# Attention by head pairs: both heads' logits alternate in pieces of 256 keys, six probability slots, pairwise waits

## What is computed

```
even: ya = sliding_window_sink_attn(aq, ak, av, sinks, slopes[:6])   # 6 heads, 2 kv heads, window 128, sink in the softmax
      yb = moba_attn(bq, bk, bv, slopes[6:])                         # 6 heads, at this length plain causal with slope * distance
      ym = memory_cross_attn(mq, mk, mv)                             # 4 heads, 256 memory keys
odd:  yc = forgetting_attn(cq, ck, cv, cf + b_f)                     # 12 heads, causal, bias from a cumulative sum
      ym = memory_cross_attn(mq, mk, mv)                             # 4 heads
both: y = concatenate(...) * silu(z);  x = x + y @ w_out
```

## Time and profile before

| | |
|---|---|
| median of 3 runs | 1302.41 us |
| profiled execution | 1304.05 us |
| its span | 1302.2 us |
| PE (matmul) busy | 1256.6 us, 97% |
| DVE busy | 640.7 us, 49% |
| ACT busy | 570.8 us, 44% |
| POOL busy | 132.2 us, 10% |
| chain that ended last | PE 93%, DVE 3%, ACT 2%, issue 1%, DMA 1% |

### The profile page before, as it was taken

One profiled execution on the slowest core, in us unless ns is written; L12 is line 12 of the kernel. 1 busy time (PEld: TensorE's weight loads), 2 busy tenths in 40 slices (PEclk: granted clock), 3 DMA queues, 4 the chain that ended last, 5 costly groups with the idle time before them and its releaser, 6 DMA issues.

```text
span 1302.2 us, 17223 instructions
## 1 busy us (share of the span) xinstructions
PE 1256.6 (97%) x6858; PEld 1014.4 (78%) x6858; DVE 640.7 (49%) x1265; ACT 570.8 (44%) x1026; POOL 132.2 (10%) x146
## 2 busy tenths in 40 slices
PE   5999999999999999999989999999799999999998
PEld 4887888889867777888978886666797889566688
DVE  4485232885343444345376637554336652445531
ACT  4433322333344455333356656554225663555520
POOL 1000000000000000000000072211300005031322
PEclk9999999999999999999989999999899999999999
DMA  5332223332312212325243321111222332021121
GB/s 170 115 98 83 95 92 96 97 98 88 98 33 65 65 33 90 119 98 178 65 98 97 95 67 34 33 44 55 65 72 92 97 98 90 24 90 57 33 67 63
DMA packets 119047, 105.77 MB, mean 81 GB/s; under 512 B 17836, under 2 KB 115500, under 8 KB 118968
## 3 DMA queue, kind: packets, MB, share of 16 engines
q1 hardware_dynamic: 117320, 98.46, 24.7%
q10 hardware_dynamic: 1648, 6.23, 1.3%
HBM read 102.55 MB, written 2.12 MB: 80 GB/s over the span
## 4 chain that ended last, share of the span: by engine, by line
PE 93%; DVE 3%; ACT 2%; issue 1%; DMA 1%; SPq 0%; DVEq 0%; ACTq 0%
PE acc L1385 26%; PE acc L1386 24%; PE acc L1387 24%; PE acc L1695 7%; PE aux L1726 3%; PE aux L1708 2%; PE aux L1539 2%; PE aux L1553 1%; ACT whi L583 1%; DVE wlo L912 1%; PE acc L1699 1%; DMA xrow<-x_dram 0%; PE aux L1603 0%; PE aux L1602 0%; PE aux L1456 0%
## 5 line engine op out<-in xcount | busy, mean ns | idle before, releaser
L1385 PE MATMUL acc<-ht_hi,whi 128*128 128x512 f32 x864 | 355.1, 411 | 8.4 <-DVE wlo L912 4.3
L1386 PE MATMUL acc<-ht_lo,whi 128*128 128x512 f32 x864 | 338.5, 392 | 0.0
L1387 PE MATMUL acc<-ht_hi,wlo 128*128 128x512 f32 x864 | 338.4, 392 | 0.0
L912 DVE TENSOR_TENSOR wlo<-raw,whi 128x2048 fp32r<-128x2048 f32 x71 | 163.4, 2304 | 148.9 <-ACT whi L583 148.8
L1385 PEld LDWEIGHTS acc<-ht_hi,whi 128*128 128x128 f32 x864 | 162.8, 188 | 67.9 <-issue 31.2
L1387 PEld LDWEIGHTS acc<-ht_hi,wlo 128*128 128x128 f32 x864 | 163.2, 189 | 35.1
L1386 PEld LDWEIGHTS acc<-ht_lo,whi 128*128 128x128 f32 x864 | 163.5, 189 | 29.7 <-issue 1.9
L583 ACT ACTIVATE whi<-raw 128x2048 fp32r<-128x2048 f32 x71 | 135.3, 1909 | 64.3 <-DMA raw<-o_w_mem_kv_dram 35.7
L529 POOL TENSOR_SCALAR whi<-raw 128x512 fp32r<-128x512 f32 x64 | 43.1, 673 | 1103.2 <-DMA raw<-e_w_in_dram 768.5
L1385 PE MATMUL acc<-whi,ht_hi 128*128 128x256 f32 x416 | 117.9, 283 | 0.0
L1386 PE MATMUL acc<-wlo,ht_hi 128*128 128x256 f32 x416 | 117.7, 283 | 0.0
(11 more groups left out here) (217 smaller groups left out, 1855.6 us busy)
## 6 DMA issues: line engine op xcount, KB each, us to landing
raw<-w_in_dram SPq DMA_DIRECT2D x72, 512.0 KB, 4.6
raw<-o_w_in_dram SPq DMA_DIRECT2D x28, 512.0 KB, 4.8
raw<-e_w_in_dram SPq DMA_DIRECT2D x18, 512.0 KB, 4.9
raw<-w_proj_pool_dram SPq DMA_DIRECT2D x8, 512.0 KB, 3.9
raw<-w_proj_mlstm_dram SPq DMA_DIRECT2D x8, 512.0 KB, 4.0
raw<-w_out_dram SPq DMA_DIRECT2D x8, 512.0 KB, 4.1
raw<-o_w_out_dram SPq DMA_DIRECT2D x8, 512.0 KB, 5.1
raw<-e_w_in_dram SPq DMA_DIRECT2D x12, 256.0 KB, 4.1
```

Of the source, the lines that this page charges most:

```text
L912: v.tensor_tensor(wlo[:, slot, :], raw[:, slot, :], whi[:, slot, :].bitcast(F32), ALU.subtract).then_inc(w_split, 1)
L1385: mm(out_, w_hi_, x_hi, start=first, stop=False)
L1386: mm(out_, w_hi_, x_lo, start=False, stop=False)
L1387: return mm(out_, w_lo_, x_hi, start=False, stop=last)
```

## The change

The loop runs over 32 pairs of jobs instead of 64 jobs. TensorE's iteration p: the logits of both heads of pair p, in pieces of at most 256 keys, a piece of the one head and a piece of the other in turn, each head in its own PSUM bank; one z product; the turning of both heads of pair p - 2; the second z product; the values of pair p - 3. It waits for both minima (memory heads: both exponentials) of pair p - 1 before the logits of pair p. VectorE makes the sink sums and inverses of a pair with one instruction each, ahead of the next pair's minima instead of behind them, and a memory pair's minima with one reduce. ScalarE scales pair p - 1 before it makes the exponentials of pair p. `pr` has six slots in place of four; `prT` is placed anew for each layer, and three constant tiles are moved to make room. Tiles 3 to 5 of the output product are also taken into the end of the loop, a pair's turning and values in between. The core of the diff:

```diff
-        pr = at("pr", [P, 4, S], R0 + 4 * K)
+        pr = at("pr", [P, 6, S], R0 + 4 * K)
...
-        def logit_bank(i):
-            return acc[:, 2 + i % 2, :]
+        def logit_bank(e):
+            return acc[:, 2 + e, :]
...
+        def pr_slot(p, e):
+            return 2 * (p % 3) + e
...
# ScalarE
+                for p in range(NP + 5):
...
+                    if z_due(p) is not None:
...
+                        nc.scalar.activation(zT[:, hu % 2, :], acc[:, hu % 2, :], ACT.Tanh, scale=0.5).then_inc(th_ready, 1)
+                    if 1 <= p <= NP:
+                        k = p - 1
+                        act.wait_ge(ri_ready, pairs_done + k + 1)
+                        for e, job in enumerate(pairs[k]):
+                            tile = pr[:, pr_slot(k, e), 0:job.keys]
+                            nc.scalar.activation(tile, tile, ACT.Copy,
+                                                 scale=stats[:, 4, 2 * k + e:2 * k + e + 1]).then_inc(norm_ready, 1)
+                    if p < NP:
+                        for e, job in enumerate(pairs[p]):
+                            i = 2 * p + e
+                            act.wait_ge(nm_ready, 2 * pairs_done + i + 1)
...
+                            nc.scalar.activation(tile, tile if job.bias is not None else logit_bank(e)[:, 0:job.keys], ACT.Exp,
+                                                 scale=-1.0, bias=stats[:, 1, i:i + 1],
+                                                 accum_out=stats[:, 2, i:i + 1]).then_inc(pr_ready, 1)
...
# VectorE
+                for p in range(NP + 6):
+                    if 1 <= p <= NP:
+                        k = p - 1
+                        dve.wait_ge(pr_ready, 2 * (done + k + 1))
+                        i = 2 * k
+                        if pairs[k][0].sink is not None:
+                            dve.wait_ge(es_ready, i + 2)
+                            step(v.tensor_tensor(stats[:, 2, i:i + 2], stats[:, 2, i:i + 2], stats[:, 3, i:i + 2], ALU.add))
+                        v.reciprocal(stats[:, 4, i:i + 2], stats[:, 2, i:i + 2]).then_inc(ri_ready, 1)
+                    if p < NP:
+                        g = done + p
+                        if pairs[p][0].bias is None:
+                            dve.wait_ge(logit_ready, g + 1)
+                            keys = pairs[p][0].keys
+                            v.tensor_reduce(stats[:, 1, 2 * p:2 * p + 2], acc[:, 2:4, 0:keys], AX.X,
+                                            ALU.min).then_inc(nm_ready, 2)
...
# TensorE
+                def logits(p):
+                    if p:
+                        pe.wait_ge(nm_ready if pairs[p - 1][0].bias is not None else pr_ready, 2 * (done + p))
+                    first = pairs[p][0]
+                    forget = first.bias is not None and first.bias[0] == "forget"
+                    for c in range(0, first.keys, 2 * P):
+                        w = min(2 * P, first.keys - c)
+                        for e, job in enumerate(pairs[p]):
+                            (qt, qp), (kt_, kp) = job.q, job.k
+                            k0 = P * job.k0 + c
+                            ins = mm(logit_bank(e)[:, c:c + w], qk[qp:qp + HD2, qt, P * job.t:P * job.t + P],
+                                     (mkT if job.bias is None else qk)[kp:kp + HD2, kt_, k0:k0 + w],
+                                     start=True, stop=not (forget and c + w == job.keys))
...
+                def turn(k):
+                    if done + k:
+                        pe.wait_ge(prT_copied, done + k)
+                    for e, job in enumerate(pairs[k]):
+                        pe.wait_ge(norm_ready, 2 * (done + k) + e + 1)
+                        for b in range(job.keys // P):
+                            ins = nc.tensor.transpose(trans_bank(e)[:, P * b:P * b + P],
+                                                      pr[:, pr_slot(k, e), P * b:P * b + P], ident[:])
+                    ins.then_inc(prT_ready, 1)
...
+                for p in range(NP + 3):
+                    if p < NP:
+                        logits(p)
+                        z_product(2 * p)
+                    if 2 <= p < NP + 2:
+                        turn(p - 2)
+                    if p < NP:
+                        z_product(2 * p + 1)
+                    elif p < NP + 2:
+                        if p == NP:
+                            pe.wait_ge(acc_free, a_out)
+                            pe.wait_ge(pr_ready, 2 * (done + NP))
+                        first = 3 * (p - NP)
+                        rows_as_tiles_come(n_out, a_out, n_out % SLOTS, a_out % 2, op_hi, op_lo, 32 + 8 * L,
+                                           range(first, first + 3))
+                    if p >= 3:
+                        weighted(p - 3)
+                done += NP
+                rows_stage(name + "_out", op_hi, op_lo, 32 + 8 * L, 1 if L == 0 else None, 6)
```

More of the change, by code:

```diff
@@ L853, in _ @@
                 az = plan[name + "_z"][1]
-                jobs = JOBS[L]
-                for i in range(len(jobs) + 7):
-                    if L == 0 and i == 52:
+                pairs = PAIRS[L]
+                for p in range(NP + 5):
+                    if L == 0 and p == 26:
                         act.dma_start(memrow[:], memv).then_inc(mem_in, 16)
[L860 to L881, removed]
+                    if z_due(p) is not None:
+                        hu = z_due(p)
                         act.wait_ge(acc_ready, 2 * az + hu + 1)
@@ L1729, in _ @@
-                done += len(jobs)
-                rows_stage(name + "_out", op_hi, op_lo, 32 + 8 * L, 1 if L == 0 else None, 3)
+                def logits(p):
[5 more added lines that the diff above has]
+                        w = min(2 * P, first.keys - c)
+                        for e, job in enumerate(pairs[p]):
+                            (qt, qp), (kt_, kp) = job.q, job.k
[3 more added lines that the diff above has]
+                                     start=True, stop=not (forget and c + w == job.keys))
+                    if forget:
+                        for e, job in enumerate(pairs[p]):
+                            ins = mm(logit_bank(e)[:, job.keys - P:job.keys], ident_r[:], causal_r[:], start=False, stop=True)
+                    ins.then_inc(logit_ready, 1)
@@ new lines, in weighted @@
+                def weighted(k):
+                    pe.wait_ge(prT_copied, done + k + 1)
+                    job = pairs[k][0]
+                    j, nb = k // TT, job.keys // P
+                    if job.t == 0 and (L or j >= 2):
+                        pe.wait_ge(t_ready, 31 + 8 * L + j)
+                    for b in range(nb):
+                        for e, one in enumerate(pairs[k]):
+                            ins = mm(out_bank(j)[HD2 * e:HD2 * e + HD2, P * job.t:P * job.t + P],
+                                     (mv if job.bias is None else vv)[:, job.k0 + b, one.v:one.v + HD2],
+                                     prT[L][2 * (k % 2) + e][:, P * b:P * b + P], start=b == 0, stop=b == nb - 1)
+                    ins.then_inc(o_ready, 1)
```

142 lines of the change are left out of this document (62 added, 80 removed).

## The result

The changed kernel takes 1252.26 us (median of 4 runs, 1250.65 to 1254.13), the kernel before 1303.01 beside it (1302.07 to 1303.86). The ratio is 0.9612, 95% interval 0.96 to 0.9624. The forecast was 1253.0 with 1244 to 1282. The profiled execution of after took 1254.13, with a span of 1252.3; before it was 1304.05 and 1302.2.

What follows compares the result with a forecast made beforehand. TensorE was taken to bound the loops through the order of its work; 25 + 30.5 - 2.3 - 1 + 1.5 - 4.5 = 49.2 off the profiled 1304.05 gives 1254.9, 1253 as a median of runs, range 1244 to 1282.

Steps and rivals of the forecast that it cites:

- Fewer changes of use: TensorE's order in both attention loops: three changes per pair instead of five, 0.39 saved in each of 64 pairs, 25 us.
- Two heads beside each other: Logits in both loops: the two heads' row halves run at a time, 143 steps x 0.213, 30.5 us saved.
- halves in turn: Rival on the logits: the two heads' passes don't overlap, 21 us of gain stay, about 1281; chance 0.13.
- Alternation costs: Rival on the logits: each pass that changes head pays a full change of use, 0.2, about 1334; chance 0.04.
- Weight loads: Logits pieces of 128 keys: four loads in a row outlast the overlapped passes, at most 4.5, half taken: 2.3 us lost.
- The rounds of DVE and ACT: Both loops: ACT's 2.95 and DVE's 2.8 per pair stay below TensorE's 3.26; the rival that they bind, 1265, had 0.13.
- the sum had 1: Sink part, while POOL makes its first split: new waits were counted as 1 us lost.
- POOL's hold: Sink adds during POOL's splits: one add per pair instead of two halves the holds, 1.5 us of old loss regained.
- The bias tile: Odd layer, next head's tile: spread lands after 3.1, wanted about 2.3 later; DVE waits 0.9 five times, TensorE loses nothing.
- The tails: Ends of both layers' loops: longer waits, 2.8 in all, and 1.7 for a clock drop, 4.5 us lost.
- a drop of the clock: Tails: TensorE's clock drops after one of the two waits, 1.7 us lost.
- The cause given for the 1.6: Tails: DVE copies two heads (0.8) before making the last z tile (0.7), so TensorE waits 1.6 instead of 0.59.

Runs made afterwards that it cites:

- e3: Changed kernel with a pair's values moved ahead of the second z product, one change of use more in 58 pairs: 1263.05 us, ratio 0.9696.
- e1: Kernel before, with only both heads' logits issued together, each whole, in every second round: 1261.91 us, ratio 0.9687.
- e2: Changed kernel with both heads' logits computed from partitions 0 to 63, the same row half: 1280.75 us, ratio 0.9832.
- e8: Changed kernel with the logits in pieces of 128 keys instead of 256, twice the weight loads: 1252.56 us, ratio 0.9617.
- e6: Changed kernel with the sink term added by two one-column TENSOR_SCALARs instead of one TENSOR_TENSOR: 1251.98 us, ratio 0.9612.
- e11: Changed kernel with the sink add as two TENSOR_SCALARs and the next heads' bias tiles made earlier, behind the fourth pair's copies: 1251.66 us, ratio 0.961.
- e7: Changed kernel with DVE's copies of the turned pair behind the z tile instead of ahead of it: 1252.34 us, ratio 0.9617.
- e10: Changed kernel with three moves at each loop's end: ACT's last tanh, DVE's last gate tile and one pair's values made earlier: 1250.9 us, ratio 0.9602.
- e4: Changed kernel with the first z product between the two heads' logits; slots, pairwise waits and merged turning stay: 1309.82 us, ratio 1.0057.

## Why the prediction was right, step by step

**Fewer changes of use, 25.** Shown. e3 prices one change at 0.19 (0.2 forecast), and e1 does so a second time; two changes fewer in 64 pairs are 24.3. A memory pair without waits says the same: 4.08 - 3.25 = 0.83, of which two steps of 0.213 are the overlap, so 0.40 (0.39 forecast). Start to start, the loops saved 43.1 in the logits, 15.9 in the turning and 1.3 in the causal tiles, and z and values took 3.9 and 0.9 more: 55.5. Without the 30.6 of e2 that is 24.9. That it meets 25 so closely is partly luck: PE's recorded waits in the loops grew by 3.7 (2.0 before logits and turning, 1.7 before the output product), while 2.0 of work moved behind the loops' ends. By the Trainium skill ("TensorEngine Tiling (Array Packing)", Key Properties) a change of tiling mode drains TensorE; the trace agrees that each change costs time, and the price is this 0.19.

**Two heads beside each other, 30.5.** Shown, e2: 30.6. The row halves work as the column halves of the values did. The rival "halves in turn" gave 1281, and e2, which forces it, took 1280.75. "Alternation costs" is refuted by the 0.63 of a pair of 256 keys.

**Weight loads, -2.3.** Wrong: they cost next to nothing. A pair of 128 keys takes 0.42, the 0.2 of a change and the 0.21 of one head's passes, and e8 doubles the loads for 0.01 in a pair of 256 keys and 0.03 in one of 512. Of the two rules of the Trainium skill weighed in the prediction, the one of "TensorE: Matmul & The Clock Gate", Part 3, that loads overlap running matmuls of another row group, is the one that these rows bear out.

**The rounds of DVE and ACT, not binding.** Right. The memory pair takes 3.25 (3.26 forecast), and PE waits for ACT's exps once in each loop, 0.2 and 0.3. In the sink part there is a remainder, the three waits at the first POOL passes: 1.8, where the sum had 1. With the adds freed (e6) the first two are down to 0.37 together, so at most that much of them is the round itself.

**POOL's hold, +1.5.** Roughly right. The sink part shows no 0.80 clock any more (both loop windows 1.00), but the hold is still there; what the higher clock gave back was not measured by itself. The prediction had it that one add per pair instead of two halves the holds. In e6 and e11 no add is held at all, and it doesn't help: whichever DVE instruction of the sensitive kinds meets a POOL pass is held, and PE's longest wait there is 0.76 in after, 0.95 in e6 and 1.03 in e11.

**The bias tile, nothing.** Nearly right, by a thinner margin than forecast. DVE waited five times as said, but 9.2 us in all, not 5 x 0.9, the longest 2.7. PE pays once, 0.34, at that longest wait. Two sizes were off. The five spreads that are waited for landed after 3.44, 3.61, 3.36, 3.08 and 4.50, not 3.1 each: the earlier trace rows give a median, and before already had one spread of 5.0. And DVE wants the tile 1.6 to 1.8 after the spread is issued, not 2.3: at a landing of 3.08 it still waited 1.28.

**The tails, -4.5.** The 2.8 for waits came, the 1.7 for a drop of the clock didn't. In each layer the wait for the last z tile was 1.44 where before had 0.59 (+0.85; +0.8 forecast), and a new one of 0.6 stands before the last tiles (0.6 forecast). The granted clock was 1.00 from 876 to 889 and from 1196 to 1210, and no run shows the term of 1.7. The +1.1 and +2.0 of "between" and "tail" in the table are not this term: they hold the moved work and leave out the wait for the z tile, which lies ahead of the loop's end. The cause given for the 1.6, DVE's copies ahead of the tile, was only half of it: ACT's head tile and tanh form a chain of the same length (e7), so both have to be moved (e10), and then the last tile's remainder is next.

**Sum.** The two profiles differ by 52.4 behind the head (55.5 in the loops less 3.1 outside them), of which the spans show 49.9 because the head of after's profiled execution was 2.5 longer. On medians the gain is 50.75. The forecast of 49.2 was 3.2 short of the 52.4. Two terms were taken off without need, 2.3 for loads and 1.7 for the clock, and the new waits in the sink part, 1.8 for 1, go the other way. That the measured 1252.26 lies within 1 us of the forecast 1253 is in part luck, since the medians differ by less than the 52.4; how long the head took in the runs without a profile is not on record.

## What to carry to other kernels

Count the changes between half-height, half-width and full use of the array in the order in which TensorE gets its work, and price one from start-to-start times (0.2 us here, as much as 128 keys of logits); then put matmuls of complementary halves directly beside each other. Whole ones will do, since cutting them into pieces brought nothing here. Buffers and pairwise waits are the means to such an order and bring nothing alone (e4); the cheap edit without them already had 43.2 of the 55.5 us (e1). Once TensorE's work is packed, the next savings of a microsecond turn into waits one instruction further on, so follow what is late next before moving anything.

## What the runs showed of the hardware

- POOL's split passes hold two kinds of DVE instruction that read and write SBUF: a TENSOR_TENSOR of 128x2 takes up to 1.10, and one of 128x1 1.28 against 0.15; two TENSOR_SCALARs of 128x256 take 1.39 and 2.05 against 0.60. The add as a TENSOR_SCALAR of 128x1 is not held (0.20 to 0.21 in e6), nor are the minima, which read PSUM (0.41 in after at 781.51, inside POOL's pass from 781.06 to 782.33). The hold comes from POOL's TENSOR_SCALAR as well as from its TENSOR_TENSOR: in after the add at 776.52 ends at 777.07, where POOL's TENSOR_SCALAR (776.44 to 777.06) ends, and in e11 it reached over both. The Trainium skill ("SBUF — State Buffer", SBUF: two separate sides) describes the shared port pair as a lock held for a whole instruction, taken by DVE instructions in a 2-port mode or with two SBUF inputs; these rows agree in which are held, though in which mode a TENSOR_SCALAR ran isn't in the trace.
- Whole 512-key matmuls of the two halves overlap even when all passes of one head are issued before the other's (e1, 1.06).
- One change between half-height, full and half-width use costs 0.19 us (e3: 58 changes, 10.8 us; e1: 3.44 against 3.25 a pair).
- Loads of weights in the two row halves stay all but hidden down to passes of 128 columns: twice the loads add 0.01 to 0.03 us to a pair of heads (e8).
- The 256 KB spread of one row's bias took between 3.1 and 5.0 us to land in the odd loop of after, and between 3.0 and 5.0 in that of before.
